# Turns of heads of a hybrid decoder step: the order of the small work between and within weight products is laid out anew

## The chip, the core and the metric

The kernel runs on one core of a Trainium2 chip. The metric is the device time of one execution in microseconds (us). A core has five engines with instruction queues of their own: TensorE (PE, matrix products, results to PSUM), VectorE (DVE), ScalarE (ACT), GpSimd (POOL) and SyncE (SP, which here only issues DMA transfers). They run on their own and meet at semaphores. An instruction waits until a semaphore has reached a value; everything behind it in the same queue waits too.

## What is computed

One layer of a decoder step, for a prompt of 512 tokens and for 8 sequences with 8 new tokens each (576 tokens together), model width 2048, everything in float32. One input projection feeds an attention group (8 heads of 128, sparse: an indexer chooses the keys) and a Mamba-2 group (16 heads of 64, state 128, chunks of 128 tokens); both outputs go through one output projection; then a gated FFN. Cut to what matters:

```python
u = rmsnorm(x, norm_attn)
q, k, v, qi, ki, wi, z, xbc, dt = split(u @ w_in)
# attention, for each head: prompt keys, or a paged cache of 512 keys and 8 new ones
logits = q @ k.T * 128 ** -0.5 + bias          # masked to the indexer's choice
att = softmax(logits) @ v
# Mamba-2, for each chunk of 128 tokens (decode: one chunk of 8)
y_intra = (C @ B.T * decay * dt) @ x
y_inter = (C @ h) * exp(acum)
h = h * exp(last) + (w * x).T @ B
y = rmsnorm((y + d_skip * x) * silu(z), ssm_norm)
h = x + concat(att, y) @ w_out
h = h + (silu(f @ w_gate) * (f @ w_up)) @ w_down   # f = rmsnorm(h)
```

Outputs are y, the new keys and values, the convolution's tails and the states `ssm_prompt` and `ssm_sample`.

## The kernel before

All engines' programs are written out by hand, with semaphores. Activations lie transposed (features on partitions, 576 tokens in the free dimension) and split into a high and a low part (`AH`, `AL`); weights are split too (`WH` by ScalarE's cast, `WL` by GpSimd's subtraction), and a product is the sum of three: high by high, high by low, low by high. One `half_unit` covers 8 of the 16 blocks of the model's width, 48 matmuls of 288 columns, for one output tile of 128 features.

**Turns.** After the projections for the indexer and for Mamba, the rest of the input projection is done head by head. Turn i (0 to 8) has on TensorE the six half products of q, k and v of head i (`product(i, n)`, n = 0 to 5) and, beside them, all the side work of attention head a = i - 1 and of the Mamba pair a. Turn 0 has products alone, turn 8 side work alone (`units=False`), turns 1 to 7 have both. The order inside a turn is that of the four functions `turn_pe`, `turn_act`, `turn_dve` and `turn_sp`, one for each engine.

**Side work of a turn on TensorE.** Prompt logits (`qk`, four tiles), logits of new tokens (`lnew`); transposes to token-major form (`by_token` of x, B, k, v: `xtok`, `btok`, `ktok`, `vtok`); C by B for the chunks (`cb0`, `cb1`); the state sum (`su`); the transposes of the eight sequences' cached keys (`kca_t`, 0 to 7) and their logits (`cached_logits`, into the bank `S`); the transposes of the old decode states (`state_t`, 0 and 1); y of the four chunks and of decode (`y_chunk`, `y_decode`); the probabilities' transposes (`probs_t`) and values (`values`) of the four query tiles; the update of the decode states (`update`, 0 and 1); the final state's transpose (`fin`); the decode probabilities' transposes (`pts`), the decode values (`pvs`) and the transpose of their result (`ats`).

**Banks.** Side results go to four PSUM banks. The list `turn` gives each result its bank; `tclaim` waits until the former result of that bank has been read, `twait` waits for the result, `tgiven` until it has been read. So the list's order binds the engines: whoever is next in a bank waits for the reader of what was there before.

**What sets the order before.** Between two half products a group of side pieces stands; only product 5 is cut, once (at k = 12, by `rest`). Cached logits are computed two sequences at a time, since the transposed keys (`kcaT`) have two buffers; the loaded keys (`kca`) have two as well, and the load of keys b waits until keys b - 2 have been transposed. The two `update` calls are apart, each with 64 rows of the block-masked `hTb`, in which the rows of other sequences are zero. The output of the decode attention is transposed (`ats`) at the turn's end.

**Loads.** SP's queue (`turn_sp`) issues in each turn six weight loads (`load_half`), the keys and values of the cache (`load_k`, `load_v`, four transfers each), biases, and towards the end of the turn eleven transfers for the next Mamba pair (`load_mamba`), the decode states `h0` the last among them. They wait for the stores of y and of the states of the turn before, which ScalarE's queue issues.

**After the turns.** Turn 8 ends with the sum of squares for Mamba's norm (`ssy`), its root and reciprocal, the splitting of the mixed activations (`mix_high`, `mix_low`), and then the output projection starts with its first `half_unit` (`C3`).

## Time and profile before

| | |
|---|---|
| median of 3 runs | 2929.3 us (2928.28 to 2938.15) |
| profiled execution, span from first to last instruction | 2922.0 us |
| the median less that span | 7.3 us |
| TensorE busy | 2762.0 us, 95% of the span |
| VectorE busy | 1768.0 us, 61% |
| ScalarE busy | 1025.9 us, 35% |
| GpSimd busy | 389.9 us, 13% |
| mean granted clock of TensorE | 0.98 |
| seven turns with products | 533.0 to 1080.9 us |
| last turn | 1080.9 to 1144.2 us |

The time shown for one execution is the device's; the profile has the span of its instructions, and no other time of that execution is given, so the sum is made against the span. The profile divides the time of each engine into busy and idle. Matmuls are pipelined, so a busy TensorE isn't one at its peak: what tells more is from which start to which start a group of matmuls runs. TensorE's clock has two levels, 2.4 GHz (1.0 in the rows) and 1.2 GHz (0.5).

### The profile page before, as it was taken

What the parts mean: (1) busy time and instruction counts of PE and PEld (TensorE: products, weight loads), DVE (VectorE), ACT (ScalarE), POOL (GpSimd) and SP (SyncE); (2) the same over time, 40 slices, a digit from 0 to 9 for tenths busy, and PEclk for the clock granted to TensorE, in tenths of its full rate; (3) what the DMA queues carried; (4) which work ended last, traced back from release to release, by engine and by line L of the source; (5) the groups of instructions that cost most, each with busy time, mean ns of one, the idle gap of its engine ahead of it and who ended that gap; (6) DMA issues with size and microseconds to landing.
All of it is one profiled execution on the core that took longest, in us unless ns stands there. A gap on an engine that the chain in (4) does not pass through costs nothing.

```text
span 2922.0 us, 49417 instructions
## 1 busy us (share of the span) xinstructions
PE 2762.0 (95%) x20329; PEld 2628.4 (90%) x20329; DVE 1768.0 (61%) x2616; ACT 1025.9 (35%) x1517; POOL 389.9 (13%) x166
## 2 busy tenths in 40 slices
PE   8999999899999988999999999999999989999997
PEld 7977898777777766998999999999999989999997
DVE  3322699354444445236877777777777787777423
ACT  5223211333333324224444344434433443443222
POOL 2322332211111101331000000000000000000231
PEclk9999999999999998999999999999999999999998
DMA  6322221655555545443333433343333464644521
GB/s 232 102 76 74 91 90 54 182 154 149 150 161 155 147 123 188 138 132 104 111 119 123 129 120 111 122 137 111 111 129 101 137 212 144 234 150 153 197 103 65
DMA packets 394448, 388.81 MB, mean 133 GB/s; under 512 B 25405, under 2 KB 354725, under 8 KB 391160
## 3 DMA queue, kind: packets, MB, share of 16 engines
q1 hardware_dynamic: 367112, 360.00, 39.3%
q10 hardware_dynamic: 27120, 25.77, 2.6%
q8 instruction: 155, 2.54, 0.4%
q14 instruction: 61, 0.50, 0.1%
HBM read 319.11 MB, written 68.00 MB: 132 GB/s over the span
## 4 chain that ended last, share of the span: by engine, by line
issue 65%; PE 22%; POOL 7%; DVE 2%; ACT 1%; DMA 1%; SPq 0%; ACTq 0%; POOLq 0%; DVEq 0%
PE PS L893 11%; PE PS L1322 5%; POOL WL L786 4%; POOL WL L811 2%; PE PS L1088 1%; PE PS L1285 1%; PE PS L1272 1%; PE PS L1059 1%; PE PS L1078 1%; PE PS L1116 1%; PE PS L1262 0%; POOL WL L819 0%; PE PS L1105 0%; DMA xin<-in_x_prompt 0%; PE PS L1278 0%
## 5 line engine op out<-in xcount | busy, mean ns | idle before, releaser
L1338 PE MATMUL PS<-xo_t,WH 128*128 128x288 f32 x2544 | 514.2, 297 | 15.6 <-DVE WL L2326 4.8
L893 PE MATMUL PS<-AH,WH 128*128 128x288 f32 (+1 forms) x2208 | 490.9, 304 | 18.1 <-POOL WL L786 4.9
L893 PE MATMUL PS<-AL,WH 128*128 128x288 f32 (+1 forms) x2208 | 480.0, 300 | 0.0
L893 PE MATMUL PS<-AH,WL 128*128 128x288 f32 (+1 forms) x2208 | 478.8, 299 | 0.0
L1338 PEld LDWEIGHTS PS<-xo_t,WH 128*128 128x128 f32 x2544 | 410.2, 189 | 17.3 <-issue 17.3
L893 PEld LDWEIGHTS PS<-AH,WH 128*128 128x128 f32 (+1 forms) x2208 | 362.2, 192 | 39.8 <-issue 32.2
L1338 PE MATMUL PS<-xo_x,WH 128*128 128x288 f32 x1936 | 389.3, 295 | 2.3 <-DVE xo_x L2414 1.0
L1338 PE MATMUL PS<-xo_t,WL 128*128 128x288 f32 x1272 | 375.9, 296 | 0.0
L893 PEld LDWEIGHTS PS<-AL,WH 128*128 128x128 f32 (+1 forms) x2208 | 362.5, 192 | 0.0
L893 PEld LDWEIGHTS PS<-AH,WL 128*128 128x128 f32 (+1 forms) x2208 | 362.2, 192 | 0.0
L1338 PEld LDWEIGHTS PS<-xo_x,WH 128*128 128x128 f32 x1936 | 309.9, 188 | 3.2 <-DVE xo_x L2414 1.2
L2326 DVE TENSOR_TENSOR WL<-WRAW,WH 128x1024 fp32r<-128x1024 f32 x201 | 245.7, 1223 | 108.9 <-ACT WH L1746 107.8
L1338 PE MATMUL PS<-xo_x,WL 128*128 128x288 f32 x968 | 284.7, 294 | 0.0
L1338 PE MATMUL PS<-xo_t,W 128*128 128x288 f32 x1944 | 275.0, 298 | 8.3 <-DVE W L2326 5.5
L1338 PEld LDWEIGHTS PS<-xo_t,W 128*128 128x128 f32 x1944 | 265.8, 190 | 9.8 <-issue 6.8
L1746 ACT CAST WH<-WRAW 128x1024 fp32r<-128x1024 f32 x201 | 211.2, 1051 | 159.5 <-PE PS L1338 152.8
L809 POOL TENSOR_TENSOR WL<-WRAW,WH 128x1024 fp32r<-128x1024 f32 x24 | 58.0, 2416 | 1485.1 <-ACT WH L800 1485.1
L1338 PEld LDWEIGHTS PS<-xo_t,WL 128*128 128x128 f32 x1272 | 241.1, 190 | 0.0
L1338 PE MATMUL PS<-xo_x,W 128*128 128x288 f32 x1416 | 197.5, 295 | 0.2 <-issue 0.2
L1338 PEld LDWEIGHTS PS<-xo_x,W 128*128 128x128 f32 x1416 | 191.3, 188 | 0.4 <-issue 0.4
L786 POOL TENSOR_TENSOR WL<-WRAW,WH 128x1024 fp32r<-128x1024 f32 (+1 forms) x58 | 139.5, 2408 | 335.2 <-ACT WH L781 335.2
L1338 PEld LDWEIGHTS PS<-xo_x,WL 128*128 128x128 f32 x968 | 182.0, 188 | 0.0
(369 smaller groups left out, 3685.5 us busy)
## 6 DMA issues: line engine op xcount, KB each, us to landing
WRAW<-in_w_gate SPq DMA_DIRECT2D x22, 2048.0 KB
WRAW<-in_w_up SPq DMA_DIRECT2D x22, 2048.0 KB
WRAW<-in_w_down SPq DMA_DIRECT2D x32, 1024.0 KB
WRAW<-in_w_in SPq DMA_DIRECT2D x14, 2048.0 KB, 8.2
raw<-in_w_in SPq DMA_DIRECT2D x48, 512.0 KB, 4.1
kca<-in_cache_k SPq DMA_DIRECT2D x256, 64.0 KB, 2.8
vca<-in_cache_v SPq DMA_DIRECT2D x256, 64.0 KB, 2.0
WRAW<-in_w_out SPq DMA_DIRECT2D x16, 1024.0 KB, 10.5
```

What stands on the lines that cost most here:

```text
L786: nc.gpsimd.tensor_tensor(WL[:, half, :, 0:w], raw[:, 8 * half:8 * half + 8, :], WH[:, half, :, 0:w].bitcast(F32), ALU.subtract).then_inc( ...
L809: nc.gpsimd.tensor_tensor(as_down(WL, h % 2), w_down_half((1, 0)[f % 2], h), as_down(WH, h % 2).bitcast(F32), ALU.subtract).then_inc(s["w_ ...
L811: nc.gpsimd.tensor_tensor(WL[:, h % 2, :, :], raw_pair((1, 0)[f % 2], h // 2)[:, 8 * (h % 2):8 * (h % 2) + 8, :], WH[:, h % 2, :, :].bitca ...
L893: last = nc.tensor.matmul(G[gslot][0:width, h, 0:HALF], wt[:, half if slot is None else slot, k % 8, 0:width], act[:, k, h * HALF:(h + 1) ...
L1059: tmade(mm(bank(f"qk{t}")[:, 0:(t + 1) * P], qT[:, t * P:(t + 1) * P], kT[:, 0:(t + 1) * P], start=True, stop=True), f"qk{t}")
L1078: last = tr(bank(f"kca{b}")[:, j * P:(j + 1) * P], kca[:, b % 2, j, :], ident[:, :])
L1088: last = mm(bank("S")[32 * c:32 * c + 32, :], qpad[:, b, :], kcaT[:, b % 2, :], start=(b < 4), stop=(b >= 4))
L1116: mm(bank("ys")[:, P + b * NQ:P + (b + 1) * NQ], hTb[:, b, :], cf[:, NP + b * NQ:NP + (b + 1) * NQ], start=True, stop=True)
L1322: last = mm(G[(slot + t) % 2][:, h, 0:HALF], wt[:, half, 2 * k + t, :], hid[:, m, k, h * HALF:(h + 1) * HALF], start=(k == 0 and wt is WH ...
L1338: last = mm(out, wt[:, k, :], act[:, m, k, :], start=(j in (0, 1, 3) and k == 0 and wt is wh and m == 0), stop=(k == 7 and wt is wl), skip ...
L1746: copy(w_high(r), operand(up, j, r)).then_inc(s["p_hi"], 1)
L2326: tt(w_low(r), operand(up, j, r), w_high(r).bitcast(F32), ALU.subtract).then_inc(s["p_lo"], 1)
```

## The change

The work is the same; its order and grouping are laid out anew in the four turn functions and in the bank list.

- Side pieces stand between half products and also within them: product 0 is cut once (prompt logits 2 and 3), product 1 once (`btok`), product 2 once (keys 0 and 1), product 3 once (logits, states 0, keys 4), product 4 twice, product 5 three times. `product` takes the function `between`, which `half_unit` calls ahead of each k.
- Cached logits are computed for four sequences at once, twice in a turn. The transposed keys get four buffers: two of them are `pt`, which is free by then (`cached_keys_t`).
- The two updates of the decode states follow each other at once, each with the 32 rows of its own four sequences in place of 64.
- The transpose of the decode attention (`decode_row`) is done at the start of the next turn, behind the first two prompt logits.
- VectorE takes v (`take(i, 2, vT)`) ahead of the state operations, and scales the decode softmax ahead of the gating.
- The decode states have loads and stores of their own on SP's queue (`load_states`, `store_states`, semaphore `h0_in`), behind `load_mamba`; before, they were the last transfer that `ssm_in` counts, and ScalarE's queue stored them.
- In turns 1 to 7, keys 4 to 7 are loaded ahead of the weight load in SP's order. In the last turn, keys 2 and 3 come first and value loads are interleaved with the key loads.
- The norm's sum `ssy` is written to a product's bank.

The core of the diff (TensorE's new order is whole; of the other engines what moves):

```diff
@@ bank list
-        turn = [("qk0", 0), ("qk1", 1), ("qk2", 0), ("qk3", 1), ("lnew", 0), ("xtok0", 2), ("xtok1", 3), ("btok0", 2), ("btok1", 3),
-                ("ktok0", 1), ("ktok1", 0), ("cb0", 2), ("cb1", 3), ("kca0", 0), ("kca1", 1), ("su", 3), ("S", 2), ("kca2", 0), ("hTb0", 3),
...
+                ("ktok0", 1), ("ktok1", 0), ("cb0", 2), ("cb1", 3), ("kca0", 0), ("kca1", 1), ("su", 3), ("kca2", 0), ("kca3", 1),
+                ("S", 2), ("hTb0", 0), ("kca4", 1), ("y0", 3), ("hTb1", 0), ("kca5", 1), ("y1", 3), ("kca6", 0), ("kca7", 1),
+                ("y2", 3), ("vtok0", 0), ("vtok1", 1), ("y3", 3), ("pt0", 0), ("ys", 3), ("pt1", 1), ("pv0", 2), ("pt2", 0), ("pv1", 2),
+                ("pt3", 1), ("us0", 3), ("us1", 0), ("pv2", 2), ("fin", 3), ("pts", 0), ("pv3", 2), ("pvs", 1), ("ats", 2)]
@@ SP
+            def store_states(i):
+
+                sp.wait_ge(s["h_done"], 2 * i)
+                sp.dma_start(bass.AP(O["ssm_sample"].tensor, (i - 1) * (P * P), [[P, P], [NM * DS * P, NB], [1, P]]), h0[:, :, :]).then_inc(s["hout"], 16)
...
+                if not units:
+                    load_k(a, 2, pages[2], i)
+                    load_k(a, 3, pages[3], i)
+                    twait(sp, "pvs", a)
+                    sp.wait_ge(s["w_used"], C3)
+                    load_v(a, 0, pages[0])
+                    for b in range(4, NB):
+                        load_k(a, b, pages[b], i)
+                        load_v(a, b - 3, pages[b - 3])
+                    for b in range(5, NB):
+                        load_v(a, b, pages[b])
+                    return
...
+                    if n == 5 and att and units:
+                        for b in range(2):
+                            load_k(a + 1, b, pages[b], i)
                     if n == 5 and mamba:
                         twait(sp, "ys", i)
                         sp.wait_ge(s["ymix"], 16 * i)
-                        sp.wait_ge(s["hout"], 16 * i)
                         sp.wait_ge(s["link_s"], 4 * i)
                         load_mamba(i)
-                    if n == 5 and att and units:
-                        for b in range(2):
-                            load_k(a + 1, b, pages[b], i)
+                        store_states(i)
+                        sp.wait_ge(s["hout"], 16 * i)
+                        load_states(i)
@@ TensorE
+                for c in range(4):
+                    last = mm(bank("S")[32 * c:32 * c + 32, :], qpad[:, 4 * m + c, :], cached_keys_t(c), start=(m == 0), stop=(m == 1))
...
+                    if i > 1:
+                        decode_row(i - 1)
+
+                def within_0(k):
+
+                    if k == 4:
+                        qk(i, 2)
+                        qk(i, 3)
+                filled(0, within_0)
...
+                def within_1(k):
+
+                    if k == 12:
+                        by_token(i, "btok", bf)
+                filled(1, within_1)
+                by_token(i, "ktok", kT)
...
+                def within_2(k):
+
+                    if k == 4:
+                        kca_t(i, 0)
+                        kca_t(i, 1)
+                filled(2, within_2)
...
+                kca_t(i, 2)
+                kca_t(i, 3)
+
+                def within_3(k):
+
+                    if k == 12:
+                        cached_logits(i, 0)
+                        state_t(i, 0)
+                        kca_t(i, 4)
+                filled(3, within_3)
+                y_chunk(i, 0)
+                state_t(i, 1)
+                kca_t(i, 5)
+
+                def within_4(k):
+
+                    if k == 3:
+                        y_chunk(i, 1)
+                        kca_t(i, 6)
+                    if k == 6:
+                        kca_t(i, 7)
+                filled(4, within_4)
+                y_chunk(i, 2)
+                by_token(i, "vtok", vT)
+                cached_logits(i, 1)
+
+                def within_5(k):
+
+                    if k == 10:
+                        y_chunk(i, 3)
+                        probs_t(i, 0)
+                    if k == 12:
+                        y_decode(i)
                         probs_t(i, 1)
                         values(i, 0)
...
+                    if k == 14:
                         probs_t(i, 2)
                         values(i, 1)
...
+                filled(5, within_5)
+                probs_t(i, 3)
+                update(i)
+                values(i, 2)
+                tclaim(pe, "fin", i)
+                pe.wait_ge(s["hT_done"], 4 * i)
+                tmade(tr(bank("fin")[:, 0:P], hT[:, 3, :], ident[:, :]), "fin")
+                tclaim(pe, "pts", i)
...
+                tmade(last, "pts")
+                values(i, 3)
...
+                for g in range(2):
+                    rows = slice(32 * g, 32 * g + 32)
+                    tmade(mm(bank(f"us{g}")[:, :], xw[rows, 4, :], hTb[rows, 4 * g:4 * g + 4, :].rearrange("p b n -> p (b n)"), start=True, stop=True), f"us{g}")
```

ScalarE's and VectorE's functions follow this order.

## Rows read from the trace of the kernel before

**Rows 1.** Windows: stretch: length, each engine's busy time (instructions), PE clock, DMA share, GB/s

```profile
533.00:1080.90 547.90, 503.03 (x3814) 427.22 (x3814) 256.62 (x639) 170.53 (x412) 97.38 (x41) 0.98 0.52 145
979.00:987.00 8.00, 7.91 (x49) 6.76 (x48) 4.75 (x9) 0.85 (x2) 1.11 (x1) 0.79 0.14 39
1080.90:1144.20 63.30, 45.30 (x262) 28.89 (x263) 34.30 (x93) 26.72 (x67) 4.68 (x2) 0.77 0.75 231
```

**Rows 2.** Waits of PE, 533.0 to 1080.9 us: total us, times, longest us

```profile
PE PS L1105 <- DVE xs L2171: 8.7, 7, 1.2
PE PS L1285 <- ACT pt L1536: 7.0, 7, 1.0
PE PS L1266 <- DVE stat L2289: 6.8, 6, 1.1
PE PS L1259 <- ACT pt L1683: 5.8, 7, 0.8
PE PS L1105 <- ACT hTb L1536: 4.8, 14, 0.3
PE PS L1158 <- ACT btok L1536: 4.4, 7, 0.9
PE PS L1171 <- DVE cbm L2220: 3.1, 6, 0.5
PE PS L1059 <- ACT attT L1536: 2.4, 6, 0.4
```

**Rows 3.** Timeline of PE in turn 6: start us, us, line, form, instructions

```profile
953.68 1.05 PE L1088 MATMUL PS<-kcaT,qpad 128*32 128x512 f32 x4
...
982.44 0.85 PE L893 MATMUL PS<-AH,WH 128*128 128x288 f32 x2
...
987.15 0.38 PE L1278 MATMUL PS<-ident,lg 128*128 128x128 f32 x2
...
987.69 1.12 PE L1272 MATMUL PS<-hTb,xw 64*128 64x512 f32 x2
988.74 0.55 PE L1278 MATMUL PS<-ident,lg 128*128 128x128 f32 x3
...
994.03 0.51 PE L893 MATMUL PS<-AH,WH 128*128 128x288 f32 x2
994.38 0.43 PE L893 MATMUL PS<-AL,WH 128*128 128x288 f32 x2
...
997.04 0.43 PE L893 MATMUL PS<-AH,WL 128*128 128x288 f32 x2
```

**Rows 4.** Timeline of PE at 157 to 159 us: prompt scores, 64 rows each

```profile
157.58 0.70 PE L988 MATMUL PS<-kit,qi 64*128 64x256 f32 x4
```

**Rows 5.** SP's timeline and the DMA view, turn 6: loads of cached keys

```profile
945.67 4.56 SPq L535 DMA_DIRECT2D kca<-in_cache_k  x8
...
kca<-in_cache_k SPq DMA_DIRECT2D x32, 64.0 KB, 2.8
```

**Rows 6.** Timeline of VectorE towards the end of turn 6

```profile
981.94 1.22 DVE L2250 TENSOR_TENSOR hTb<-btok,own 64x1024 f32<-64x1024 f32 x1
...
988.85 1.12 DVE L2265 SCALAR_TENSOR_TENSOR h<-h,els,PS 128x128 f32<-128x128 f32 x4 [2.65 <-PE PS L1272]
...
997.50 0.76 DVE L2129 TENSOR_TENSOR vT<-PS,rstd 128x576 f32<-128x576 f32 x1 [0.61 <-PE PS L893]
```

**Rows 7.** SP's timeline and the DMA view: first and last of ten Mamba loads

```profile
920.79 0.33 SPq L514 DMA_DIRECT2D xs<-xcS  x1
...
926.35 0.49 SPq L521 DMA_DIRECT2D dcol<-in_d_skip  x1
...
dcol<-in_d_skip SPq DMA_DIRECT2D x2, 0.2 KB, 5.3
```

**Rows 8.** Last turn: SP's value loads, and PE's wait for keys

```profile
1087.80 8.87 SPq L539 DMA_DIRECT2D vca<-in_cache_v  x16
...
PE PS L1078 <- DMA kca<-in_cache_k: 4.5, 4, 2.1
```

624 lines of the change are left out of this document (267 added, 357 removed), and 2 rows, old and new, of the table turn.

## Prediction

> **What bounds the kernel now.** I read the page first: by its line for TensorE (PE), in the table above, PE is busy for 95% of the span, so only time that PE idles, repeats or spends at the low clock can be won. The windows then say where that time lies inside the turns of heads. The seven turns with weight products (533.0 to 1080.9 us, 78.3 us each) have PE busy for 503.0 of 547.9 us, 44.9 us idle, at a mean granted clock of 0.98; the eighth, without products, takes 63.3 us, PE busy 45.3, clock 0.77 [rows 1]. Everything else in the program is left as it is. The view of waits splits the idle time: 43 us in eight groups, nearly all seven times the same wait of 0.3 to 1.2 us [rows 2]. None waits for weights, so the splitting of the weights (ScalarE cast, GpSimd subtraction) is not on the path there. A turn is therefore: six half products, the side work on PE beside them, 6.3 us of short waits, and one dip of the clock.
>
> **Part by part, per turn and times seven.**
>
> *Waits whose cause gets a product in between.* The second y chunk waited for the chain of masks and additions on VectorE behind the first (8.7 us in all); values 3 waited for the copy of its probabilities (7.0); the decode values waited for ScalarE's copy of theirs (5.8); the y chunk behind a state transpose waited for its eviction (4.8); the chunk products waited for the token-major B (4.4) and the state sum for the masks' buffer (3.1) [rows 2]. In the new order half a product or more lies between cause and user in each case but two: values 3 now has the state update, values 2 and the decode transposes in front of it, and it itself covers the copy for the decode values. I take all of it as gone: 33.8 us. What is next late I price below.
>
> *The border of two turns.* VectorE needs two operations on the decode output, then PE transposes it and ScalarE evicts it before the first logits may run: 6.8 + 2.4 = 9.2 us over six borders [rows 2], 1.5 us each. Now the first logits run during VectorE's two operations and the transpose writes another bank. The second logits still wait until VectorE has released bank 1, so about 0.6 us of idling stays: gain 0.9 x 6 = 5.4 us.
>
> *Cached logits, four at a time.* Each call is a product with 32 columns of the array. Two together took 1.05 us for their four instructions [rows 3]; two streams of 512 at the pace of one. Four go to four different column groups, so I price four at the 1.05 us of two: two groups in place of four pairs, 2.1 us saved, less 0.1 for the longer tail: 2.0 x 7 = 14 us. Bounds: 0 (no further overlap) and 2.1. The Trainium skill (TensorE: Matmul & The Clock Gate, Part 3, "Measured speedup vs the span model") is less kind: four packed tiles of 512 ran 3.07 times as fast as one by one. By it, as an estimate with the 1.05 us above as one product's time, four would take 1.37 us, and this term would be 10 us in place of 14.
>
> *Both state updates at once.* One update runs 1.05 us from its start to the next piece's (987.69 to 988.74) [rows 3]. The two now use 32 rows each, in different row groups and banks. The prompt scores do the like with 64 rows: four instructions, which are two products of 256 columns, in 0.70 us [rows 4]; I take the overlap as full: 1.05 x 7 = 7.3 us.
>
> *The clock.* In every turn the granted clock falls once, to the 1.2 GHz level, after a stretch with transposes, the 16 tiny decode products and logits: 0.79 mean over 979 to 987 us [rows 1]. The 24 matmuls behind it took 4.71 us (982.44 to 987.15); at full clock a pair takes 0.266 us (ten pairs from 994.38 to 997.04), and 24 take 3.3 with the entry [rows 3]. That is 1.4 us a turn, 1.7 with the logits. The tiny products now lie inside product 5, with matmuls of a product before and after, but another stretch without a product grows from two of 7 us to one of some 11 us (end of product 5 to product 0). I take half of the cost as gone: 0.85 x 7 = 6 us; ends 0 and 12.
>
> *More cuts.* Products are cut at nine places in place of one. Going back into a product costs about 0.1 us: its first pair took 0.35 us (994.03 to 994.38) in place of 0.266 [rows 3]. 8 x 0.1 x 7 = 5.6 us against; ends 0 and 11.
>
> *New wait 1: cached keys 2 and 3.* There are two key buffers. The loads of keys 2 and 3 wait until keys 0 and 1 have been transposed, which now happens in the middle of product 2. From there to the transposes of keys 2 and 3 PE has 24 matmuls (3.2 us) and the state sum (0.9). The queue takes 4.56 us to issue the eight loads, and one lands 2.8 us after its issue (median) [rows 5]: keys 2 are there 0.15 + 1.8 + 2.8 = 4.8 us after the start of issue, keys 3 after 4.2 + 2.8 = 7.0. PE would stand ready for keys 3 about 5.3 us after. I take 1.7 us of idling a turn: 12 us against. Ends 0.5 (two loads' issue at the shortest) and 2.5. Keys 4 to 7 have more room, since their loads are moved ahead of the weight load on SP's queue, and half a product each lies before them.
>
> *New wait 2: banks behind VectorE.* The final state's transpose takes bank 3 behind update 0, and the decode transposes take bank 0 behind update 1; both are free only when VectorE has read them. VectorE has by then a backlog: decode y, the block mask (1.22), softmax scaling, the gating, the squares and their sum, the take of vT (0.76 for 576 columns, as each of these passes), then twice four state operations (1.12) [rows 6]. Laid end to end from the decode y, vT is taken about 1.2 us after product 5's end, bank 3 is free at 2.7, bank 0 at 4.0; PE, with probabilities 3, both updates (1.1) and values 2, is ready for them at 2.3 and 2.5 plus. So 0.5 and 1.1 us idle, and 0.3 behind the decode copy: 1.9 x 7 = 13.3 us against, ends 0.5 and 3. It also means that most of what the joined updates save on PE is given back here; that is in the sum, since both stand in it.
>
> *New wait 3: the Mamba loads.* They no longer wait for the state's store, but the store of y that they do wait for is now issued behind values 3. Ten issues take 6 us (920.79 to 926.35 and 0.5), and the last lands 5.3 us after its issue: 11 us after the first [rows 7], so at about 10.5 us of the new turn. PE wants xs at about 9.9: 0.6 x 6 = 3.6 us against; ends 0 and 2. The states themselves (store, wait, load) then hold SP's queue for some 8 us; behind them stands the fourth weight load, whose cast is due 7 us later, so it costs nothing. If that cover went, the casts and product 3 would be late by the difference.
>
> *The last turn.* SP now gives keys 2 and 3 ahead of the 16 value loads, but those, which were issued in the 8.87 us before the keys were due [rows 8], come interleaved between keys 4 to 7, four value loads (1.9 us) ahead of each. PE waited 4.5 us for keys [rows 8]; I work out 12. The Mamba data comes 1 us later. Against these 8.5 us stand the logits (2 to 3 us, since part runs at the low clock), the updates (1 to 2), the waits of y, of values 3 and of the decode values (1.2, 1.0 and 0.8 us at the longest [rows 2]) and the softmax scaling, now ahead of the gating (1 to 2), less 1 to 2 for the banks. I take 0, ends -6 and +5.
>
> **Sum.** Gains 33.8 + 5.4 + 14 + 7.3 + 6 = 66.5; costs 5.6 + 12 + 13.3 + 3.6 = 34.5; net 32 us. The profiled execution's span is 2922.0 us, so 2890 after. The median of the runs is 2929.3, 7.3 us above that span; I keep this distance: **2897 us**. A turn falls from 78.3 to 73.7 us.
>
> **Rivals.** (a) *The new waits do not appear and the clock stays up*: key loads land at their shortest, VectorE's backlog is shorter, no dip. Against it: each new wait comes from rows. 2897 - 29 = 2868 us. (b) *The new waits are twice as long*, since the queues that feed them delay each other: 2897 + 29 = 2926 us, no change. For it: three of the four new waits are chained, a late turn start delays the stores which the next loads wait for. Against it: half a product lies between most of them. (c) *The grouping does not overlap*: logits and updates take as long as before. 21 us lost, some 17 of them visible: 2914 us. Against it [rows 4], and the 32 instructions of the decode values. (d) *Slower: the low clock spreads.* Place: from the end of product 5 to product 0, and the cut products with transposes in the middle. The low level doubles a matmul's 0.133 us. It decides when it covers more than 4.6 us (35 matmuls) more of product time in each turn than now; if a whole product of 48 ran low in each turn, that is 48 x 0.133 x 7 = 45 us: 2942 us. For it: in the last turn, which has side work alone, the mean clock is 0.77 [rows 1]. Against it: the dips of the seven turns ended within one product. The Trainium skill (same page, Part 4: PE-mode transpose) says that transposes don't count as busy for the clock as matmuls do; by it the pieces put into products are worse for the clock than their time, which is this rival's case.
>
> **How the numbers follow.** Forecast, 2882 to 2910 us: 0.60. (a) 0.13, (b) 0.08, (c) 0.06, (d) 0.04; 0.09 for the rest, mostly between forecast and (b). Half a per cent of 2929, 14.6 us, is about what a measurement of this kernel can tell from no change: faster by more 0.84, within 0.10, slower 0.06. The range, 2874 to 2914, takes in the ends of the unknown terms short of their common extremes, and the edges of (a) and (c).
>
> **What would show it.** In the profile after: turns of 72 to 75 us; the logits' eight instructions in about 1.1 us, the updates' four in 1.1; no idle time before the chunk products and y chunks; idle time before keys 2 and 3 put down to their loads, before the final state's and the decode transposes put down to VectorE's state operations; xs waiting for its loads by less than 1 us; in the last turn waits for keys up, not down. The prediction is wrong if PE waits for weights inside the turns, if turns lie above 76 us, or if the rest of the program moves.

## The result, and the profile after

The changed kernel takes **2899.4 us** (median of four runs, 2891.6 to 2905.4) where the kernel before took 2928.8 us beside it: 0.9906 of the time, 95% interval 0.9878 to 0.9934. A second set of six runs, made with its variants below, gave 2898.5 us and 0.9910 (0.9886 to 0.9933). The forecast was 2897. The sum behind it is another matter: most of its terms came out near what was worked out, but the cached keys, the Mamba loads, the banks, the clock and the last turn did not.

The profiled execution of after took 2905.4 us, its span is 2903.6. First the windows (stretch: length, busy time of PE, PEld, DVE, ACT, POOL, then PE clock, DMA share, GB/s): the seven turns with products, the last turn, and turn 3 alone.

```profile
534.70:1056.70 522.00, 484.25 (x3817) 431.57 (x3817) 277.20 (x637) 171.22 (x412) 98.16 (x41) 0.96 0.54 151
1056.70:1127.50 70.80, 43.26 (x260) 30.51 (x261) 34.20 (x93) 27.23 (x67) 4.67 (x2) 0.72 0.67 207
681.10:756.40 75.30, 69.59 (x546) 62.04 (x546) 39.77 (x93) 24.53 (x59) 14.35 (x6) 0.95 0.56 159
```

Against [rows 1] the seven turns fell by 25.9 us: 18.8 us of busy time and 7.1 of idle time (44.9 to 37.8), at a lower clock. The last turn rose by 7.5 us: its busy time fell by 2.0, its idle time rose from 18.0 to 27.5. All else moved by 2 us (before the turns 534.7 against 533.0 us, behind them 1776 against 1778).

The waits of PE in the seven turns (who waits, for whom: total us, times, longest us):

```profile
PE PS L1103 <- DMA kca<-in_cache_k: 17.9, 11, 3.6
PE PS L1270 <- DVE h L2289: 6.2, 7, 0.9
PE PS L1093 <- DMA dcol<-in_d_skip: 4.4, 4, 1.7
PE PS L1132 <- DVE xs L2191: 3.2, 13, 0.3
PE PS L1084 <- DVE attS L2298: 3.1, 7, 0.4
PE PS L1264 <- DVE h L2289: 2.4, 7, 0.3
```

None of the groups of [rows 2] is left except small remains of two: the y chunks (at most 0.3 us each time) and the border (at most 0.4). The cached keys alone take nearly half of the idle time. PE's timeline in turn 3 (start us, us, line, form, instructions, and idle time in brackets) shows what the regrouped instructions cost and what surrounds the key wait:

```profile
703.60 0.50 PE L918 MATMUL PS<-AH,WH 128*128 128x288 f32 x2
703.94 0.42 PE L918 MATMUL PS<-AL,WH 128*128 128x288 f32 x2
704.20 0.43 PE L918 MATMUL PS<-AH,WL 128*128 128x288 f32 x2
...
711.24 1.86 PE L1103 MATMUL PS<-ident,kca 128*128 128x128 f32 x8 [3.33 <-DMA kca<-in_cache_k]
712.75 0.83 PE L918 MATMUL PS<-AH,WH 128*128 128x288 f32 x2
...
717.17 0.62 PE L1114 MATMUL PS<-kcaT,qpad 128*32 128x512 f32 x2
...
718.17 0.66 PE L1124 MATMUL PS<-ident,h 128*128 128x128 f32 x4
...
745.93 1.13 PE L1298 MATMUL PS<-hTb,xw 32*128 32x512 f32 x4
746.99 0.94 PE L1311 MATMUL PS<-pt,vtok 128*128 128x128 f32 x6
...
748.27 0.33 PE L1264 MATMUL PS<-ident,hT 128*128 128x128 f32 x1 [0.34 <-DVE h L2289]
749.48 1.12 PE L1270 MATMUL PS<-ident,lgs 128*128 128x128 f32 x4 [0.89 <-DVE h L2289]
```

The eight instructions of a group of cached logits run from 717.17 to 718.17: 1.00 us. The four of both updates run from 745.93 to 746.99: 1.06 us. A product taken up again needs 0.34 us for its first pair (703.60 to 703.94) and 0.26 for the next. And behind the key wait of 3.33 us the same eight transposes of 128 rows take 1.86 us that take 1.04 at full clock, as the run with pairs shows below.

SP's queue from the end of turn 2 into turn 3 (the border is at 681.1 us) shows where the keys come from:

```profile
679.76 0.33 SPq L512 DMA_DIRECT2D xs<-xcS  x1
...
685.73 0.47 SPq L519 DMA_DIRECT2D dcol<-in_d_skip  x1
686.25 0.60 SPq L528 DMA_DIRECT2D ssm_sample<-h  x1
691.43 0.40 SPq L523 DMA_DIRECT2D h<-in_state_ssm  x1
691.87 0.58 SPq L484 DMA_DIRECT2D raw<-in_w_in  x1
...
703.17 1.06 SPq L484 DMA_DIRECT2D raw<-in_w_in  x2
704.34 5.07 SPq L541 DMA_DIRECT2D kca<-in_cache_k  x8
```

Between the store of the states (`ssm_sample`) and their load (`h`) the queue stands still for 4.6 us. Everything behind is late by it: two weight loads of 512 KB each go out at 703.17 us, directly ahead of the eight loads of keys 2 and 3. The transposes that free the two buffers had ended by about 703.6, so the queue came to these loads some 0.7 us late and, behind the two weight loads, into busy DMA engines: from 703 to 711.9 us they were busy for 0.9 of the time or more in most slices of the DMA view.

In the last turn the longest waits of PE are:

```profile
PE PS L1103 <- DMA kca<-in_cache_k: 10.6, 5, 3.8
PE PS L1093 <- DMA dcol<-in_d_skip: 5.3, 1, 5.3
PE PS L1152 <- DVE stat L2301: 3.9, 1, 3.9
```

### The profile page after: what moved, and what is told of

Read it like the earlier page. It is cut to its first block, busy times and chain, and to the rows that moved or that the text cites. A ratio compares the mean times of both kernels' runs of the same rounds, so it can differ in the third digit from the quotient of the medians.

```text
span 2903.6 us, 49432 instructions
## 1 busy us (share of the span) xinstructions
PE 2748.0 (95%) x20329; PEld 2641.8 (91%) x20329; DVE 1787.6 (62%) x2616; ACT 1027.1 (35%) x1517; POOL 391.8 (13%) x166
## 4 chain that ended last, share of the span: by engine, by line
issue 66%; PE 16%; POOL 7%; SPq 4%; DMA 3%; DVE 3%; ACT 0%; ACTq 0%; POOLq 0%; DVEq 0%
PE PS L918 6%; PE PS L1350 5%; POOL WL L807 4%; POOL WL L832 2%; SPq L545 2%; SPq L541 1%; DMA ssm_sample<-h 1%; DMA kca<-in_cache_k 1%; DVE mt L2182 1%; PE PS L1103 1%; DVE ex L2174 1%; DMA mixS<-xs 1%; PE PS L1311 1%; DVE h L2289 1%; PE PS L1143 1%
## 5 line engine op out<-in xcount | busy, mean ns | idle before, releaser
L1366 PE MATMUL PS<-xo_t,WH 128*128 128x288 f32 x2544 | 517.0, 298 | 14.1 <-DVE WL L2338 3.7
```

What stands on the lines that cost most here:

```text
L1366: last = mm(out, wt[:, k, :], act[:, m, k, :], start=(j in (0, 1, 3) and k == 0 and wt is wh and m == 0), stop=(k == 7 and wt is wl), skip ...
```

## The experiments

All times are medians beside runs of the kernel before on the same chip; a ratio is to that kernel. "Turns" is the sum of the seven turns with products, which was 522.0 us in the profile of after. "Low" is how long the trace's clock records show the lower level within the turns; it was 27.3 us in the kernel before and 41.0 us in after. The windows and waits of a run come from one profile each.

### Is the wait for keys the queue's lateness?

The forecast priced this wait by issue and landing alone (1.7 us a turn), with a queue that is free. Theory A: the queue is late and crowded. Rival B: the distance from buffer release to use is simply too short.

**keys_first**

```diff
@@ turn_sp, for n in range(6)
+                    if n == 3 and att:
+                        for b in (2, 3):
+                            load_k(a, b, pages[b], i)
                     if units and (more or n < 3) and not (n < 3 and isinstance(i, int) and i == 0):
                         load_half(i if n < 3 else i + 1, (n + 3) % 6)
...
-                    if n == 3 and att:
-                        for b in (2, 3):
-                            load_k(a, b, pages[b], i)
```

> The changed kernel, with the loads of cached keys 2 and 3 issued ahead of the weight load of the next head (one 512 KB transfer) instead of behind it. In the changed kernel PE waits 17.9 us for keys in the seven turns, 3.1 to 3.6 us at a time in turns 2, 3, 5 and 6. Theory A (the keys' transfers stand behind weight transfers on the DMA engines and on SP's queue, because the queue has come late to this point): one of two weight transfers moves behind the keys, so each long wait falls by 1 to 1.5 us, the total to 9 to 13 us. Theory B (the wait is only the time from the release of the key buffer to landing, as the prediction had it): the queue reaches the keys at the same time, and the total stays at 16 to 19 us. Time against the changed kernel: A -5 us or a little more, B 0.

Measured: 2882.2 us (2876.6 to 2883.8), 0.9852 (0.9834 to 0.9871). The turns' window and the key wait:

```profile
532.90:1029.00 496.10, 466.84 (x3817) 415.05 (x3817) 276.14 (x638) 171.22 (x412) 98.21 (x41) 1.00 0.57 159
```

```profile
PE PS L1103 <- DMA kca<-in_cache_k: 7.9, 13, 1.3
```

The key wait fell by 10 us, the turns by 25.9. The larger part isn't idle time: the same 3817 instructions were busy for 466.8 us in place of 484.3, at clock 1.00 in place of 0.96. (Beside the second profile of the changed kernel, `again` below, it is the other way round: the turns fell by 17.0 us, 9.3 of it key waits and 6.9 busy time.)

**states_later**

```diff
@@ turn_sp
                 if not units:
+                    sp.wait_ge(s["hout"], 16 * a)
+                    load_states(a)
...
+                    if n == 2 and att and i > 1:
+                        sp.wait_ge(s["hout"], 16 * a)
+                        load_states(a)
...
                         store_states(i)
-                        sp.wait_ge(s["hout"], 16 * i)
-                        load_states(i)
```

> The changed kernel, with SP's wait for the landing of the states' store and the load of the new states moved from the turn's border to behind the third weight load of the next turn. Theory A (SP's queue is held some 4 to 5 us at the border, and all that follows, weight loads and values, reaches the keys 2 and 3 late, with two weight transfers just ahead of them): the queue gets to keys 2 and 3 before their buffer is free, the long waits of turns 2 to 6 fall from 3.1 to 3.6 us to 1 to 2 us, as in turns 1 and 7, the total from 17.9 to 6 to 10 us. Theory B (release to landing alone): total stays at 16 to 19 us. With A also one dip of the clock per turn (the one behind the wait for keys, 1.7 us each) may go. Time against the changed kernel: A -8 to -17 us, B 0.

Measured: 2881.4 us (2878.4 to 2893.6), 0.9861 (0.9832 to 0.9891). Turns 498.7, key waits 8.0, busy 469.4 at clock 0.99, low for 6.8 us. Here the order of keys and weights is that of the changed kernel; only the queue no longer stands at the state's store. So either of two remedies takes the same 10 us of key wait. Neither helps the Mamba loads: PE's wait for them was 6.2 us in keys_first and 6.1 us here, against 4.4 and 7.0 in the two profiles of the changed kernel.

**keys_early**: PE transposes keys 0 and 1 three steps earlier in product 2.

```diff
@@ turn_pe, within_2
-                    if k == 4:
+                    if k == 1:
                         kca_t(i, 0)
```

> The changed kernel, with the transposes of keys 0 and 1 put at k = 1 of product 2 instead of k = 4, so the key buffers come free 2.4 us earlier. Theory B (buffer release sets the landing of keys 2 and 3): every wait for keys falls by 2.4 us, the total in the seven turns from 17.9 to under 4 us. Theory A (the queue comes late, whenever the buffer is free): turns 2 to 6 keep their waits within 0.7 us, only turns 1 and 7 lose theirs; total 14 to 17 us. Time against the changed kernel: B -15 us, A -1 to -3.

Measured: 2893.9 us (2890.7 to 2903.4), 0.9895 (0.9866 to 0.9923). Turns 514.5, key waits 15.7, low for 27.3 us. 2.4 us more room in every turn between release and use gave 2.2 us of the 17.9 in all. B, which wanted under 4 us left, falls.

### Why is the queue late?

**y_store**: on ScalarE the store of y, for which `load_mamba` waits, goes ahead of five evictions and the store of the final state.

```diff
@@ turn_act
                 probs(3)
+                act.wait_ge(s["y_done"], i)
+                act.dma_start(bass.AP(mixS.tensor, a * (P * NT) + 8 * P * NT, [[NT, P], [1, NT]]), xs[:, :]).then_inc(s["ymix"], 16)
                 outputs(2)
...
                 act.dma_start(bass.AP(O["ssm_prompt"].tensor, a * (P * P), [[P, P], [1, P]]), fin).then_inc(s["finout"], 16)
-                act.wait_ge(s["y_done"], i)
-                act.dma_start(bass.AP(mixS.tensor, a * (P * NT) + 8 * P * NT, [[NT, P], [1, NT]]), xs[:, :]).then_inc(s["ymix"], 16)
```

> Edit on the changed kernel: ScalarE issues the store of y directly behind its fourth pair of probabilities, not behind the third group of decode outputs. Theory A (the waits before the Mamba products, xs against the DMA of the decay columns, 4.4 us in the turns and 5.3 us in the last turn, are the time at which the loads behind that store start on the queues): the store is out 1 to 2 us earlier, the waits fall to under 2 us in the turns. Rival B (the Mamba loads are late because the synchronous engine's queue stands at the state's landing, whatever the y store does): the waits stay at 4 to 5 us, and the time within 2 us of the changed kernel's. I hold B more likely (.6), since the two earlier experiments that emptied that queue moved the turns by 24 us. Rival C: ScalarE now waits for y ahead of its outputs and all of the decode part slips: turns' sum over 525 us.

Measured: **2869.7 us** (2866.3 to 2878.6), 0.9818 (0.9794 to 0.9843). I had put .6 on the rival that it changes nothing; it was the largest effect of any single edit. In the changed kernel VectorE has y ready at 744.7 us, and ScalarE's queue stores it 8.3 us later (VectorE's and ScalarE's timelines of after, turn 3):

```profile
743.93 0.76 DVE L2277 TENSOR_TENSOR xs<-xs,sz 128x576 f32<-128x576 f32 x1
```

```profile
752.57 0.36 ACTq L1702 DMA_DIRECT2D ssm_prompt<-cbm  x1
752.96 1.10 ACTq L1704 DMA_DIRECT2D mixS<-xs  x1
```

With the edit: the turns' window, PE's key wait and SP's queue (border of turns 2 and 3 at 672.4 us):

```profile
532.80:1021.70 488.90, 468.30 (x3817) 417.39 (x3817) 276.61 (x638) 171.73 (x412) 98.25 (x41) 0.99 0.59 165
```

```profile
PE PS L1103 <- DMA kca<-in_cache_k: 5.1, 9, 0.9
```

```profile
665.73 0.33 SPq L512 DMA_DIRECT2D xs<-xcS  x1
...
676.56 0.40 SPq L523 DMA_DIRECT2D h<-in_state_ssm  x1
...
686.91 5.96 SPq L484 DMA_DIRECT2D raw<-in_w_in  x2
694.40 3.75 SPq L541 DMA_DIRECT2D kca<-in_cache_k  x8
```

The Mamba loads begin 6.7 us before the border in place of 1.3, the state's load follows 4.2 us after it in place of 10.3. The standstill at the store is still there (from 671.6 to 676.6 us) but does no harm now: by 692.9 us both weight loads are issued, and the queue then waits 1.4 us for PE's transposes, so that the eight key loads go out at their buffers' release, with one weight load 1.9 us ahead of them in place of two directly ahead. The wait for Mamba data is gone from the list. So three experiments on three different places of one chain (the store that opens it, the standstill in it, the order at its end) each take away 10 to 13 of its 17.9 us. The chain, not the distance from release to use, sets that part; the 5.1 to 8.0 us that stay may be the distance's. From the DMA view, the eight loads of keys 2 and 3 land a median of 3.7 us after issue in after (703 to 711.9 us). In this run it is 2.0 us over fourteen loads, six of them of keys 4 and 5 (694 to 703 us), and 2.2 us for the eight of keys 2 and 3 alone (694 to 698.3 us):

```profile
kca<-in_cache_k SPq DMA_DIRECT2D x8, 64.0 KB, 3.7
```

```profile
kca<-in_cache_k SPq DMA_DIRECT2D x14, 64.0 KB, 2.0
```

### Are the banks' waits VectorE's backlog?

**squares**

```diff
@@ turn_dve
-                dve.wait_ge(s["y_done"], i)
-                ls(tt(ea[:, :], xs[:, :], xs[:, :], ALU.mult))
-                ls(tt(ssq[:, :], ssq[:, :], ea[:, :], ALU.add))
-                ls.end()
...
                     cp(stat[:, 2, 6:7], els[:, 0:1]).then_inc(s["h_done"], 1)
+                dve.wait_ge(s["y_done"], i)
+                ls(tt(ea[:, :], xs[:, :], xs[:, :], ALU.mult))
+                ls(tt(ssq[:, :], ssq[:, :], ea[:, :], ALU.add))
+                ls.end()
```

> Edit on the changed kernel: on VectorE the squares of y and their sum are done behind the state operations of a turn instead of ahead of them. Theory A (the waits of TensorE before the decoded tokens' probability transposes, 6.2 us over seven turns, and before the final states' transposes, 2.4 us, are VectorE's backlog, as the forecast's banks 3/0 term said): both waits fall to 0 to 2 us together, the turns' sum (522.0 us in the changed kernel) falls by 5 to 8 us, the time by the same, ratio to the kernel before .988 or less against .9906. Rival B (VectorE isn't what is late there; the banks come free later for another reason, ScalarE's exponentials say): both waits stay over 5 us together and the time stays within 2 us. Rival C: the waits go, but the square sum is now late at the border and the low-clock windows (41.0 us in the turns) grow or shift: the sum falls by under 3 us.

Measured: 2904.1 us (2898.3 to 2909.3), 0.9932 (0.9907 to 0.9957): no gain. The two waits are 6.2 and 2.4 us as before. VectorE's timeline says why:

```profile
742.94 0.76 DVE L2149 TENSOR_TENSOR vT<-PS,rstd 128x576 f32<-128x576 f32 x1 [0.93 <-PE PS L918]
744.43 1.12 DVE L2285 SCALAR_TENSOR_TENSOR h<-h,els,PS 128x128 f32<-128x128 f32 x4 [0.73 <-PE PS L1298]
...
745.65 1.11 DVE L2285 SCALAR_TENSOR_TENSOR h<-h,els,PS 128x128 f32<-128x128 f32 x4
```

VectorE is now idle for 0.73 us ahead of the state operations and waits for PE's update, which starts 1.16 us before them (743.27 to 744.43), exactly as in the changed kernel (745.93 to 747.09). There the backlog ended at 747.06: both causes were ready at the same moment, so taking one away shows nothing. My theory A named one of two, and B was right in its number and wrong in its reason.

**upd_recip**: (1) the updates ahead of the fourth probability transposes; (2) in the last turn, the reciprocal of the norm behind the attention's output.

```diff
@@ turn_pe
-                probs_t(i, 3)
                 update(i)
+                probs_t(i, 3)
@@ turn_dve
-                if not units:
-                    dve.wait_ge(s["ssy_taken"], 2)
-                    nc.vector.reciprocal(rstd[:, :, :], rstd[:, :, :]).then_inc(s["ry_done"], 1)
...
                 cp(stat[:, 2, 5:6], hmask[:, 0:1]).then_inc(s["att_s"], 1)
+                if not units:
+                    dve.wait_ge(s["ssy_taken"], 2)
+                    nc.vector.reciprocal(rstd[:, :, :], rstd[:, :, :]).then_inc(s["ry_done"], 1)
```

> Two edits on the changed kernel that touch different stretches. (1) In every turn TensorE issues the two state updates ahead of the fourth probability transposes, not behind them. (2) In the last turn VectorE's reciprocal of the norm (3.75 us) stands behind the attention's output operations instead of ahead of them. Theory A for (1): the squares' run kept the waits at .34 and .89 us although VectorE had become idle, so they are the length of the chain from the updates over VectorE's eight state operations to the transposes; .6 us more work between them (four transposes) takes .6 us off the .89 and all of the .34 can't go as well: together 1.23 falls to about .65 a turn, 4 us over seven. Rival B: the whole of it is VectorE's lateness again and nothing changes. Theory A for (2): the wait of 3.9 us before the last transposes of the attention falls to under 1 us, the last turn goes from 70.8 to 67 to 68 us. Rival B for (2): the square root's operands arrive late too and the reciprocal then delays the first output tiles: the last turn stays, or the stretch behind it grows by 3 us. Time by A: 6 to 8 us under the changed kernel's on this chip.

Measured: 2892.4 us (2888.3 to 2899.3), 0.9889 (0.9866 to 0.9912), 6.1 us under the changed kernel beside it, with overlapping intervals. Its turns are 507.2 us against 513.1; 3.9 us of that are key waits (13.3 against 17.2) and 1.4 waits for Mamba data (5.6 against 7.0), which I can't tie to either edit. Of (1)'s 4 us only 0.5 came: the waits are 6.2 and 1.9 us. PE's update was early now and VectorE's backlog set the start of the state operations, the other of the two causes. The 0.9 us before the decode transposes can't change while PE waits before the final state's at all, since it is the second group of four state operations (1.2 us) less one transpose (0.3). For (2): the wait before the attention's transpose fell from 2.7 us (3.9 in after) to 1.1, but the one before the first output tiles rose from 1.5 to 4.1: the last turn stayed at 70.2. Rival B of (2) holds: the reciprocal is needed right afterwards, and its place decides only who waits for it.

### What did the grouping of instructions give?

**pairs**: the cached logits again in two pairs with a piece between.

```diff
@@ turn_pe
-                        cached_logits(i, 0)
+                        cached_logits(i, 0, 0)
                         state_t(i, 0)
+                        cached_logits(i, 0, 1)
...
+                cached_logits(i, 1, 0)
                 by_token(i, "vtok", vT)
-                cached_logits(i, 1)
+                cached_logits(i, 1, 1)
```

> Edit on the changed kernel: the cached logits are issued as two pairs with another piece between them, as in the kernel before, in place of four at a time. Everything else is of the changed kernel. Theory A (the forecast's: eight instructions of four column groups take 1.00 us, the same eight in pairs 2.0 us, so 1.0 us twice in a turn): TensorE's turns become 1.5 to 2.2 us longer, the sum 522.0 goes to 532 to 537 us, the time up by 12 to 16 us, ratio about .995. Rival B (the gain of the logits is taken back, since the waits before the cached keys, 17.9 us in the turns, absorb what is saved ahead of them): the key waits fall by up to 8 us and the time is only 3 to 7 us longer.

Measured: 2909.6 us (2907.0 to 2912.6), 0.9944 (0.9924 to 0.9965). The turns' window, and in PE's timeline a transpose group at full clock and one pair:

```profile
533.60:1060.80 527.20, 488.35 (x3817) 423.53 (x3817) 278.41 (x638) 171.08 (x412) 97.95 (x41) 0.98 0.54 150
```

```profile
705.14 1.04 PE L1103 MATMUL PS<-ident,kca 128*128 128x128 f32 x8
...
718.75 1.05 PE L1114 MATMUL PS<-kcaT,qpad 128*32 128x512 f32 x4
719.73 0.66 PE L1126 MATMUL PS<-ident,h 128*128 128x128 f32 x4
```

A pair takes 0.98 us (718.75 to 719.73), four took 1.00. The profile of the changed kernel to set beside it is that of `again` below, which had the same clock of 0.98 and was low for the same 17.1 us: 488.4 less 473.8 is 14.6 us of busy time, and the turns are longer by 14.1 us. The key waits are 17.5 against 17.2 us, so rival B falls. The medians, from two sets of runs, differ by 11.1 us.

**upd_before**: on the kernel before, both updates at the place of the second, 32 rows each.

```diff
@@ turn_pe
-                    if mamba:
-                        update(i, 0)
...
                     if mamba:
-                        update(i, 1)
+                        update(i)
```

> Edit on the kernel before: only the two state updates are put together, at the place of the second, each on 32 rows of its own, as in the changed kernel. Theory A (the forecast's: two updates of four instructions each cost half as much when issued together, 1.04 us a turn): turns' sum falls from 547.8 us by 5 to 8 us, ratio .9975 to .998. Rival B (alone it pays nothing: the first update filled a place in which TensorE then waits, and VectorE gets the first update's bank later): sum within 2 us of before, ratio .999 to 1.001. Rival C: VectorE's state operations start later and the border's waits grow: slower by 3 us or more.

Measured: 2921.5 us (2915.0 to 2935.2), 0.9993 (0.9977 to 1.001): nothing. In the turns' window and the waits:

```profile
541.60:1090.50 548.90, 499.29 (x3814) 426.30 (x3814) 255.83 (x638) 171.28 (x412) 97.37 (x41) 0.97 0.52 145
```

```profile
PE PS L1279 <- ACT pt L1537: 4.4, 7, 0.6
```

PE is busy for 3.7 us less than in [rows 1], and a wait of 4.4 us has appeared that [rows 2] don't have: the first update had filled the time in which ScalarE copies the probabilities. B holds. The saved instruction time became a wait in the same place; it is only worth something where the order gives PE other work there.

### The last turn's loads, and the best version

**last_old**: the loads of the last turn in their order of before.

```diff
@@ turn_sp, if not units
-                    load_k(a, 2, pages[2], i)
-                    load_k(a, 3, pages[3], i)
                     twait(sp, "pvs", a)
                     sp.wait_ge(s["w_used"], C3)
-                    load_v(a, 0, pages[0])
-                    for b in range(4, NB):
-                        load_k(a, b, pages[b], i)
-                        load_v(a, b - 3, pages[b - 3])
-                    for b in range(5, NB):
-                        load_v(a, b, pages[b])
+                    for b in range(4):
+                        load_v(a, b, pages[b])
+                    for b in range(2, 6):
+                        load_k(a, b, pages[b], i)
+                    for b in range(4, 6):
+                        load_v(a, b, pages[b])
+                    for b in range(6, NB):
+                        load_k(a, b, pages[b], i)
+                    for b in range(6, NB):
+                        load_v(a, b, pages[b])
```

> The changed kernel with the last turn's loads in the order of the kernel before: values 0 to 3, then keys 2 to 5, values 4 and 5, keys 6 and 7, values 6 and 7. The last turn (from the last but one border to the output projection's start) took 70.8 us in the changed kernel and 63.4 before. Theory A (the interleaved value loads, 1.9 us of queue each, hold the keys back): the waits for keys fall from 10.6 us to 5 to 7, and the last turn by 4 to 6 us. Rival (the last turn is longer because the Mamba data comes late and the reciprocal on VectorE holds back the decode output, both of which stay): keys' waits fall but the turn gets under 2 us shorter.

Measured: 2897.8 us (2894.4 to 2905.6), 0.9909 (0.9884 to 0.9934). The last turn fell from 70.8 to 67.0 us, but the key waits in it only from 10.6 to 9.5; the Mamba wait was 4.4 against 5.3. It stands clear of the other profiles with the new order and late Mamba loads, whose last turns took 70.1 to 71.6 us. The whole kernel's time does not show it.

**again** is the changed kernel itself, beside upd_recip, best and best_new.

> The changed kernel itself, once more, beside its variants on the same chip. Its time should be 2890 to 2906 us and its ratio .988 to .993. It decides one more thing: the low-clock windows in the seven turns were 41.0 us in its profile, and 0 to 27 us in variants of it. Theory A (the windows follow from how the waits of a turn lie): its turns have 35 us or more again and their sum is 518 to 526 us. Rival B (the windows come and go between executions of one kernel): under 25 us this time, with the same key waits of 16 to 19 us.

Measured: 2898.5 us (2896.6 to 2909.0), 0.9910 (0.9886 to 0.9933). The turns' window and the key wait:

```profile
538.00:1051.10 513.10, 473.76 (x3817) 421.96 (x3817) 276.25 (x637) 171.23 (x412) 98.12 (x41) 0.98 0.55 154
```

```profile
PE PS L1103 <- DMA kca<-in_cache_k: 17.2, 11, 3.6
```

The waits are nearly those of after; the clock is not (low for 17.1 us against 41.0), and busy time is 10.5 us less with it. B was right on the point that I put it to: one profile's clock is not a property of the kernel to within 10 us.

**best** joins y_store, keys_first, upd_recip and last_old; **best_new** is the same without last_old.

> The changed kernel with the edits that helped and the two of the run above: the store of y behind the fourth pair of probabilities, the third and fourth cached keys' loads ahead of the next weights, updates ahead of the fourth probability transposes, the norm's reciprocal behind the attention's output, and the last turn's loads in the order of the kernel before. Theory A: the store's edit alone gave turns of 488.9 us with 5.1 us of waits for keys and 6.8 us of low clock; the others take 3 to 4 (keys), 4 (updates) and, in the last turn, 3 to 6 us more: 2852 to 2862 us, ratio .976 to .979. Rival B (the keys' edit gives nothing once the store is early, as both removed the same lateness): 2860 to 2866 us.

> As the run above, but with the last turn's loads in the changed kernel's order. It prices that part of the change where the Mamba loads are early. Theory A (the new order costs the last turn time whatever stands ahead, as keys 2 and 3 are asked for while the earlier ones are still in use, and values are spread among keys): the last turn is 2 to 5 us longer than above, all of it before the cached keys' transposes. Rival B (it cost only because of the late loads ahead of it): equal within 1 us.

Measured: best **2863.6 us** (2862.8 to 2869.5), 0.9793 (0.9769 to 0.9817); best_new 2865.1 us (2858.1 to 2872.7), 0.9789 (0.9762 to 0.9815). Windows of the turns and of the last turn of best, then the last turn of best_new with its key wait:

```profile
535.00:1020.10 485.10, 465.27 (x3817) 414.28 (x3817) 276.01 (x638) 171.63 (x412) 98.24 (x41) 1.00 0.59 166
1020.10:1084.30 64.20, 42.11 (x261) 29.99 (x261) 33.04 (x93) 27.09 (x67) 4.66 (x2) 0.72 0.67 205
```

```profile
1021.00:1087.70 66.70, 40.71 (x261) 28.51 (x261) 33.06 (x92) 27.29 (x67) 4.67 (x2) 0.76 0.64 198
```

```profile
PE PS L1103 <- DMA kca<-in_cache_k: 11.0, 5, 3.0
```

Both beat the changed kernel by 33 to 35 us and the kernel before by 2%. Best lies just above my 2852 to 2862, in the range of its rival B, and the key waits of 5.1 us are those of y_store alone: once the store is early, the order of keys and weights takes nothing more off them. With the new order of its loads the last turn is 2.5 us longer (key waits 11.0 against 7.3 us in best, Mamba data early in both), as it was 3.8 us longer with the Mamba data late (last_old). So that part of the change seems to cost a little in either surroundings; in the whole kernel's time it is below what was measured.

## Why the prediction was right in the sum and not in its terms

**The seven turns together.** Forecast 32 us less; measured 25.9 in after and 34.8 in again. The terms as worked out below give some 18 and 26 us. For the gain stand the short waits and the border (36.7), the logits (14.6) and the updates (7.3); against it the cuts (4.5, an estimate), the banks (8.6), the keys (17.9 and 17.2) and the Mamba loads (4.4 and 7.0); the clock is -5 in one and +5 in the other. So some 8 us of gain in either profile belong to no term of the forecast, and most of them are busy time. Where it comes from was not tested. One place can be seen: four transposes of keys are busy for 0.60 us in the profile of before when a wait follows them (955.60 us), and in keys_first, where a product follows them, that product starts 0.35 us after them (707.59 to 707.94). So a wait that goes may take with it some of the busy time ahead of it.

**The short waits.** Forecast 33.8 us gone; of the six groups 3.2 us is left, at the y chunks [rows 2]. The border: forecast 3.6 us of rest (0.6 a turn), measured 3.1. Right.

**Logits four at a time.** Forecast 1.05 us for eight instructions and 14 us in all; measured 1.00 us, and 14.6 us by pairs. The price came from the row of two in [rows 3] and the reading that 32 columns of the array are a quarter. The factor of 3.07 that the Trainium skill gives (TensorE: Matmul & The Clock Gate, Part 3, "Measured speedup vs the span model") is for four tiles packed by rows, and these four lie side by side in columns. By it, as an estimate, the term would have been 10 us, which was too low here: the pair took 0.98 us and the four 1.00.

**Updates at once.** Forecast 1.05 us for both, measured 1.06. That most of it is given back was in the sum, and upd_before shows that it can be all of it.

**Banks behind VectorE.** Forecast 13.3 us, measured 8.6 (6.2 and 2.4). The two waits came where they were forecast, the size was too large, and the reason half right: laid end to end, VectorE's backlog sets the first state operation, but so does PE's own update 1.16 us before it. I had followed only one of the two to that instruction.

**Cuts.** Forecast 0.1 us each; the first pair behind a cut took 0.34 us against 0.26, so 0.08. Their sum was not measured by itself.

**Cached keys: the failed step.** Forecast 12 us, measured 17.9 and 17.2. The term took issue and landing from [rows 5], where the queue is on time (it had just waited 2.3 us for GpSimd to free a weight buffer), and the sentence that the state's store, wait and load "then hold SP's queue for some 8 us", which "costs nothing", looked only at the first weight load behind it and its cast. What stood behind that were sixteen value loads, three more weight loads, and the keys. Each place of that chain, changed alone, takes 10 to 13 us of the key wait away. What then stays, 5.1 to 8.0 us, is less than the 12 that issue and landing alone were priced at: with the queue on time (y_store, turn 3) the eight loads took 3.75 us to issue in place of 4.56, and landed after 2.2 us in place of 2.8. So the term had two errors of opposite sign, the missing lateness (10 to 13 us) and a distance priced too high, and its miss of 5 to 6 us is their difference.

**Mamba loads.** Forecast 3.6 us, measured 4.4 and 7.0. The term had the right cause, "the store of y that they do wait for is now issued behind values 3", and no price for its further effects: the same lateness delays all of SP's queue. y_store puts that sentence's price at 29 us of the whole kernel (2898.5 to 2869.7 us; the two come from different sets of runs, beside the same kernel before at 2924.0 and 2924.9 us). Not all of it is lost against the kernel before: there the loads began 3.7 us before the border, with the edit 6.7 and in the changed kernel 1.3.

**The clock.** Forecast a gain of 6 us. With clock 1.00 the turns' instructions are busy for 466.8 us (keys_first); so the low clock costs 17.4 us in after and 6.9 in again. The forecast put its cost before at 12, which fits the 27.3 us of low clock there (41.0 us cost 17.4 in after). That makes -5 and +5 in place of the 6 forecast. The reason, that a product around the tiny matmuls keeps the clock up, is not borne out as far as it was meant: full clock came only where the key waits were short, and no run tested whether the one brings the other.

**The last turn: the other failed step.** Forecast 0, ends -6 and +5; measured +7.5 and +6.9, outside. The key waits were priced well (12, measured 10.6 and 11.0). But I set 8.5 us of gains against them, and busy time fell by only 2.0 us: PE stands idle for 27.5 of 70.8 us there, so what gets shorter is mostly followed by a longer wait. The Mamba loads' lateness, 1 us in the forecast, was 3.2 us (a wait of 5.3 against 2.1 before). And PE waits 3.9 us behind VectorE's reciprocal before the attention's transpose, where it had waited 1.8 us before (the reciprocal stood ahead of the attention's output in that kernel too). Moving it only moved the wait (upd_recip). I had not followed VectorE's queue through this turn.

**Span and median.** I added 7.3 us as a distance between span and time. The distance is 1.8 us in the profiled execution of after; the rest was scatter, since the runs of one set and kernel lie 6 to 20 us apart. The span forecast was 2890, the spans are 2903.6 and 2897.7. The median was met with some help: the 7.3 us, of which 5.5 do not exist, made up for most of the 7 lost in the last turn: that is luck. Median against median, which needs no such distance, the change gave 29.4 and 25.5 us where the sum had 32.

**Rivals.** (a) and (c) are refuted by the waits and by pairs. (b), new waits twice as long since the queues delay each other, has the right mechanism: measured, the key waits are 1.5 times the forecast. All new waits together are 30.9 and 32.8 us against 28.9 in the sum, since the banks' came out smaller. (d), the low clock, came about in a small part: 17.4 us against the 12 put down for before, so some 5 in the worse of the two profiles, not 45.

## What the runs showed of the clock

Over the profiled executions of the changed kernel and its variants, the turns fall in two groups. Where the key waits are 13 to 18 us (after and again, squares, keys_early, last_old, upd_recip, pairs), the lower level lasts 17 to 41 us; where they are 5 to 8 us (keys_first, states_later, y_store, best, best_new), 0 to 7 us. In turn 3 of after one of the places is the stretch behind the key wait: the lower level begins at 711.7 us, the eight transposes at 711.24 us took 1.86 us, and the pair at 712.75 stands 0.63 us ahead of the next. The other is at 749.3 us, among the waits before the final state's and the decode transposes, which hardly differ between the runs. A microsecond less of key wait went with up to 2.6 us of the turns' sum in keys_first (25.9 us for 10.0), though against the second profile it is 1.8 (17.0 for 9.3). Which of the two figures holds in an execution can't be forecast from one profile. Why the clock falls in some turns and not in others with the same waits stays open, and so does whether the key wait is what makes it fall.

## What to carry to other kernels

A wait or a store that is moved on one engine's queue has to be followed through every DMA issued behind whatever it releases, up to the last one that someone waits for, and not only to the next. When an engine's instruction starts, ask for all of its causes and their times: where two are ready within 0.1 us, taking away either one shows nothing. Time saved on an engine that idles a few instructions later is a gain only if something else can fill the place. A total that comes out right is no proof of its terms: here errors of 5 to 8 us stood on both sides.
